# Neighbourhood attention in pairs of heads, with products between its turns

## The chip, the cores and the metric

One core of a Trainium2 chip runs the kernel. The metric is the device time of one execution in microseconds. The kernel before took 3163.59 us (median of three runs, 3157.02 to 3165.70).

## The reference, cut to what matters

The program runs two blocks over 256 latent tokens `x` and 256 context tokens, with 1024 features, everything in fp32. The first block has two layers of SwiGLU feed-forward, a mixer, and feed-forward again. The second block has two layers: latent attention (8 heads) with an MLP, and neighbourhood attention (16 heads of 64) with an MLP. The change touches the two attentions, and the order of the feed-forward tiles. Neighbourhood attention is:

```python
s_lat = jnp.einsum('bqhd,bkhd->bhqk', q_row, k_strip).astype(jnp.float32) * scale + bias
s_lat = jnp.where(mask, s_lat, -jnp.inf)
s_ctx = jnp.einsum('bqhd,bkhd->bhqk', q_row, kc).astype(jnp.float32) * scale
p = jax.nn.softmax(jnp.concatenate([s_ctx, s_lat], -1), axis=-1).astype(v.dtype)
return jnp.einsum('bhqk,bkhd->bqhd', p, jnp.concatenate([vc, v_strip], 1))
```

The grid has 4 rows of 64 columns, so the strip is the whole latent sequence; the bias comes from a table of relative positions per head. The output of all heads goes through `w_o`. Latent attention is a softmax attention over context and latent keys, with query, key and value made from low-rank vectors (`uq`, `uk`, and `mla_v`) and a rotary part.

## The kernel before, in words

All activations lie feature-major: 8 tiles of 128 features by 512 tokens, context first. A weight is read as a slab of 128 x 1024 (SP's queue, seven slots), and split in two fp32r parts: high by ScalarE (L1300), low by VectorE (L1706). An activation has a high and a low part as well, and a product is three matmuls (L2192, L2193, L2194). A slab feeds 24 of them. `schedule` (L860) walks one hand-written order of steps, `order` (L736), and every engine's program takes its own steps out of it; so each engine works in that order, and waits by semaphores. When a slab is used up ("done"), the slab seven further is fetched and the slab five further is split.

In the feed-forward stages `ffn_pieces` (L464) makes the hidden tiles of a chunk (the sizes are in `SIZES`, L166), then the eight down products of that chunk, then the next chunk. The dot products of the modulation (two VectorE operations of 1024 elements each) are put between.

`beside` (L564) lays pieces of products between the turns of an attention: the turn's steps, then the copies of the piece before ("late"), then the products of one piece, then the next unit's scores. `pair_turns` (L680) gives turns of a pair of heads: turn i normalises unit i-1, transposes unit i-2, and weighs the values when a pair's last unit is through. For latent attention (`mla_steps`, L697) a unit is a pair of heads and one tile of 128 queries: scores of both heads in two of three banks (L2542, and the rotary part with the rows 0 to 63 and 64 to 127 of the array, L2545), max by VectorE (L2104), exponential by ScalarE (L1606), reciprocal and scaling by VectorE (L2110, L2114), transposes by TensorE (L2367), copy by ScalarE (L1626), weighing (L2394). Its pieces have the banks 4 and 5: `both` (L693) joins two products into one piece, and the list is

```python
pieces = [both(*q1), both(uk[0], uk[1]), both(uk[2], uk[3]), both(*q2), both(*q3), v[0], v[1], None, None, None, None, *outs]
```

with 19 turns for 19 entries; `outs` is the half of the output product over the first four feature tiles.

For neighbourhood attention, the keys (`na_k`), queries (`na_q`) and all values (`na_tm`, copied with their bias by VectorE at L1861) are made first. `na_steps` (L729) then runs 32 units, one head and 128 queries each, with `skewed`:

```python
yield from skewed(32, ("na_scores", "na_normalise", None, None, "na_turn"), more)
```

A unit: scores of one head in 64 rows of the array (L2555); ScalarE copies the context half with the scale (L1634); VectorE scales the latent half and adds the bias into SBUF (L2126), and takes the max (L2119); ScalarE's exponential (L1613); reciprocal by VectorE (L2134); scaling by POOL (L1232); four transposes (L2348) and a copy (L1462). Each second unit weighs the head's values (L2384, one bank per parity), ScalarE copies the result (L1479), and for each second head its high and low parts are made (L1359, L1784). The bias of a head is loaded by two DMAs of SP (L1116), reversed by a POOL copy (L1244) and masked by a second POOL operation (L1246), one head ahead of its use. The output product (`na_out`, 8 slabs) follows behind the last head, with the residual added by VectorE (L1833).

## Time and profile before

| | |
|---|---|
| median of three runs | 3163.59 us |
| profiled execution | 3168.26 us |
| its span | 3166.5 us |
| TensorE matmul busy | 2887.7 us (91%) |
| TensorE weight load busy | 2367.5 us (75%) |
| VectorE busy | 1975.9 us (62%) |
| ScalarE busy | 1174.8 us (37%) |
| POOL busy | 417.7 us (13%) |
| mean granted TensorE clock | 0.946 |

Busy times overlap, and a matmul's end is modelled, so the busy share of TensorE says only whether it had work. The stretches in the section with the rows are cut by hand from the start of a stage's first matmul to the start of what follows its last. PEclk is the clock that TensorE was granted, as a share of 2.4 GHz.

### The profile page before, as it was taken

What the parts mean: (1) busy time and instruction counts of PE and PEld (TensorE: products, weight loads), DVE (VectorE), ACT (ScalarE), POOL (GpSimd) and SP (SyncE); (2) the same over time, 40 slices, a digit from 0 to 9 for tenths busy, and PEclk for the clock granted to TensorE, in tenths of its full rate; (3) what the DMA queues carried; (4) which work ended last, traced back from release to release, by engine and by line L of the source; (5) the groups of instructions that cost most, each with busy time, mean ns of one, the idle gap of its engine ahead of it and who ended that gap; (6) DMA issues with size and microseconds to landing.
All of it is one profiled execution on the core that took longest, in us unless ns stands there. A gap on an engine that the chain in (4) does not pass through costs nothing.

```text
span 3166.5 us, 38256 instructions
## 1 busy us (share of the span) xinstructions
PE 2887.7 (91%) x15166; PEld 2367.5 (75%) x15166; DVE 1975.9 (62%) x3242; ACT 1174.8 (37%) x1953; POOL 417.7 (13%) x460
## 2 busy tenths in 40 slices
PE   3899999988899998999998799988899998988797
PEld 2788887545788887888887699855678887845797
DVE  7888855645678857878555765533566764433554
ACT  3222234443422234232355554423442223335552
POOL 0000010322100010000101110100310003035201
PEclk7999999978999999999999899988999999989898
DMA  6555522101355634555332255310144432332353
GB/s 245 193 193 206 180 85 87 54 27 40 137 196 194 213 110 163 199 199 200 107 105 67 67 187 187 114 53 20 60 140 160 162 138 73 107 76 41 130 187 107
DMA packets 125281, 412.13 MB, mean 130 GB/s; under 512 B 25088, under 2 KB 27136, under 8 KB 124464
## 3 DMA queue, kind: packets, MB, share of 16 engines
q1 hardware_dynamic: 109552, 353.07, 33.0%
q0 software_dynamic: 15552, 56.63, 5.1%
q8 instruction: 120, 1.97, 0.2%
q14 instruction: 57, 0.47, 0.0%
HBM read 408.60 MB, written 1.05 MB: 129 GB/s over the span
## 4 chain that ended last, share of the span: by engine, by line
PE 80%; DVE 8%; ACT 7%; issue 2%; POOL 2%; DMA 1%; POOLq 0%; SPq 0%; ACTq 0%; DVEq 0%
PE bank L2192 25%; PE bank L2193 24%; PE bank L2194 24%; PE bank L2394 2%; POOL sb_temp L1168 1%; DVE sb_split_low L1706 1%; ACT sb_split_high L1300 1%; DVE sb_temp L1770 1%; DVE sb_temp L1720 1%; DVE sb_h_low L1776 1%; DVE sb_rstd L1762 1%; PE bank L2384 1%; ACT sb_temp L1613 1%; PE bank L2542 1%; ACT sb_x_res L1370 1%
## 5 line engine op out<-in xcount | busy, mean ns | idle before, releaser
L2192 PE MATMUL bank<-sb_h_high,sb_split_high 128*128 128x256 f32 (+1 forms) x3040 | 1066.6, 351 | 119.6 <-DVE sb_h_low L1776 47.9
L2193 PE MATMUL bank<-sb_h_low,sb_split_high 128*128 128x256 f32 (+1 forms) x3040 | 1042.8, 343 | 0.0
L2194 PE MATMUL bank<-sb_h_high,sb_split_low 128*128 128x256 f32 (+1 forms) x3040 | 1041.7, 343 | 0.0
L1706 DVE TENSOR_TENSOR sb_split_low<-sb_raw,sb_split_high 128x1024 fp32r<-128x1024 f32 x515 | 636.1, 1241 | 231.9 <-ACT sb_split_high L1300 228.3
L2192 PEld LDWEIGHTS bank<-sb_h_high,sb_split_high 128*128 128x128 f32 x3040 | 592.1, 195 | 213.4 <-issue 69.8
L1300 ACT ACTIVATE sb_split_high<-sb_raw 128x1024 fp32r<-128x1024 f32 x515 | 536.6, 1051 | 344.9 <-DMA sb_raw<-weights 344.8
L2193 PEld LDWEIGHTS bank<-sb_h_low,sb_split_high 128*128 128x128 f32 x3040 | 594.0, 195 | 67.2 <-issue 0.5
L2194 PEld LDWEIGHTS bank<-sb_h_high,sb_split_low 128*128 128x128 f32 x3040 | 593.0, 195 | 68.1
L1720 DVE CUSTOM_DVE_ANT_0 sb_temp<-sb_ada_ffn,sb_cond_ffn 128x1024 bf16<-128x1024 f32 x408 | 479.2, 1218 | 12.0 <-ACT sb_cond_ffn L1304 7.9
L1833 DVE SCALAR_TENSOR_TENSOR sb_x_res<-bank,sb_gates,sb_x_res 128x256 f32<-128x256 f32 x312 | 140.1, 477 | 265.5 <-PE bank L2194 265.2
L2192 PE MATMUL bank<-sb_hidden_high_ffn,sb_split_high 128*128 128x512 f32 (+1 forms) x788 | 272.7, 346 | 0.0
L2193 PE MATMUL bank<-sb_hidden_low_ffn,sb_split_high 128*128 128x512 f32 (+1 forms) x788 | 272.1, 345 | 0.0
L2194 PE MATMUL bank<-sb_hidden_high_ffn,sb_split_low 128*128 128x512 f32 (+1 forms) x788 | 272.0, 345 | 0.0
L1378 ACT ACTIVATE sb_temp<-bank 128x256 f32<-128x256 f32 (+1 forms) x163 | 80.3, 493 | 362.0 <-PE bank L2194 361.9
L1391 ACT ACTIVATE sb_hidden_high_ffn<-sb_temp 128x512 fp32r<-128x512 f32 (+1 forms) x94 | 52.1, 555 | 356.2 <-DVE sb_temp L1811 356.2
L2192 PE MATMUL bank<-sb_hidden_high_mlp,sb_split_high 128*128 128x256 f32 (+1 forms) x552 | 180.9, 328 | 0.0
L2193 PE MATMUL bank<-sb_hidden_low_mlp,sb_split_high 128*128 128x256 f32 (+1 forms) x552 | 180.5, 327 | 0.0
L2194 PE MATMUL bank<-sb_hidden_high_mlp,sb_split_low 128*128 128x256 f32 (+1 forms) x552 | 180.4, 327 | 0.0
L1148 POOL DMA_DIRECT2D sb_ada_ffn<-ada x90 | 47.8, 532 | 897.1 <-DVE sb_ada_col L1720 897.1
L2193 PEld LDWEIGHTS bank<-sb_hidden_low_ffn,sb_split_high 128*128 128x128 f32 x788 | 148.3, 188 | 19.9
L2192 PEld LDWEIGHTS bank<-sb_hidden_high_ffn,sb_split_high 128*128 128x128 f32 x788 | 148.3, 188 | 19.9
L2194 PEld LDWEIGHTS bank<-sb_hidden_high_ffn,sb_split_low 128*128 128x128 f32 x788 | 148.3, 188 | 19.8
(265 smaller groups left out, 3088.9 us busy)
## 6 DMA issues: line engine op xcount, KB each, us to landing
sb_raw<-weights SPq DMA_DIRECT2D x515, 512.0 KB, 3.3
sb_ada_ffn<-ada SPq DMA_DIRECT2D x114, 512.0 KB, 4.3
sb_ada_ffn<-ada POOLq DMA_DIRECT2D x90, 512.0 KB, 3.5
sb_ada_mlp<-ada POOLq DMA_DIRECT2D x18, 512.0 KB, 3.4
sb_ada_mlp<-ada SPq DMA_DIRECT2D x18, 512.0 KB, 4.2
sb_cond_ffn<-cond SPq DMA_DIRECT2D x3, 1024.0 KB, 5.1
sb_na_raw<-na_rpb SPq DMA_DIRECT2D x32, 96.0 KB, 5.8
sb_x_res<-tokens SPq DMA_DIRECT2D x1, 2048.0 KB, 15.2
```

The source lines that it names most:

```text
L1148: lane.do.dma_start(m.ada[f][i][:, :], m.w["ada"][n, :, :]).then_inc(*lane.mark(ada_signal(n), n, step=16))
L1168: do.tensor_tensor(acc, other if k == 1 else acc, new, ALU.add).then_inc(*pool.mark("added", (kind, tag, k, p)))
L1300: do.activation(m.high[s % SLOTS][:, :], m.raw[s % SLOTS][:, :], identity).then_inc(*act.mark("split_high", s))
L1378: do.activation(m.temp[h % 2][:, COLS[p]], src, func).then_inc(*act.mark(name, (f, h, p)))
L1391: do.activation(m.hidden[f][i][:, m.hidden_cols(f, p)], m.temp[h % 2][:, COLS[p]], identity).then_inc(*act.mark("hidden_high", (f, h, p)))
L1706: do.tensor_tensor(m.low[i][:, :], m.raw[i][:, :], m.high[i][:, :].bitcast(F32), ALU.subtract).then_inc(*dve.mark("split_low", s))
L1720: do.tensor_tensor_reduce(out=m.junk(s), in0=m.ada[f][i][:, :], in1=m.cond[f][:, s, :], scale=1.0, scalar=0.0, op0=ALU.mult, op1=ALU.add, ...
L1833: do.scalar_tensor_tensor(x, m.bank[bank][:, bank_cols(p, s)], m.gates[:, k, s:s + 1], x, ALU.mult, ALU.add).then_inc(*dve.mark("x_new", ( ...
L2192: do.matmul(out, ah, bh, start=start and j == 0, stop=False)
L2193: do.matmul(out, ah, bl, start=False, stop=False)
L2194: last = do.matmul(out, al, bh, start=False, stop=stop and j == len(terms) - 1)
L2394: last = do.matmul(m.bank[bank][:, c], vals[:, kt, col + hd * P:col + (hd + 1) * P], m.big[stage][:, at + kt, c], start=kt == 0, stop=kt = ...
```

## The change

- Neighbourhood attention runs in `pair_turns` as latent attention does: 16 units of two heads and 128 queries in 19 turns. The scores of both heads are in different rows of the array and in two of three banks; the query's scale is applied where the query is copied (all by VectorE). VectorE adds the bias in place in PSUM, takes the max from PSUM, and scales by the reciprocal; POOL has no part in it any more. The two heads of a pair are weighed in one bank, in alternating matmuls on different output columns, with one copy of 128 partitions.
- The bias of a pair is loaded (four DMAs) one turn ahead of the turn that makes it, which VectorE does with one operation for each head, reversed and masked at once.
- Before the turns: five query slabs and half the values (`na_v0`). Between the turns: three query slabs, the other values (`na_v1`, eight pieces of two slabs and one token tile), an empty entry, and the output product over the first four feature tiles. Behind: its second half. The first four tiles of the attention's result are put as high and low parts in turn 11.
- Latent attention: `uq` 1 goes ahead of the turns, each piece has one bank, the value pieces take one token tile; the slabs' order follows, and four tiles of the result may be put earlier (`H_LAST_FIRST`).
- Feed-forward in chunks: the first hidden tile of the next chunk is made before the down products (`AHEAD`), with one more buffer for a hidden tile.

```diff
-          ("mla_uk1", 1), ("mla_uq2", 2), ("mla_v1", 1), ("mla_out", 8), ("mlp0", 64),
-          ("na_fm", 16), ("na_tm", 8), ("na_out", 8), ("mlp1", 64)]
+          ("mla_uq2", 2), ("mla_uk1", 1), ("mla_v1", 1), ("mla_out", 8), ("mlp0", 64),
+          ("na_k", 8), ("na_q", 5), ("na_v0", 4), ("na_q5", 3), ("na_v1", 4), ("na_out", 8), ("mlp1", 64)]
 N_SLABS = sum(n for _, n in STREAM)
+AHEAD = 1
...
-      "na_tm": (NA_V, 0, 4, (0, 1))}
-OUT_HALVES = {"even_out": (4, 0), "odd_out": (0, 4), "mla_out": (0, 4)}
+      "na_v0": (NA_V, 0, 4, (0,)), "na_v1": (NA_V, 0, 4, (1,))}
+OUT_HALVES = {"even_out": (4, 0), "odd_out": (0, 4), "mla_out": (0, 4), "na_out": (0, 4)}
...
+def ups_at(f, c):
+    return min(chunk_at(f, c) + AHEAD, sum(SIZES[f])) if c else 0
 def down_slab(f, c, block):
-    return SLAB0[f] + chunk_at(f, c + 1) * n_up(f) + chunk_at(f, c) + block // 8
+    return SLAB0[f] + ups_at(f, c + 1) * n_up(f) + chunk_at(f, c) + block // 8
+def n_hidden(f):
+    return max(SIZES[f]) + (AHEAD if len(SIZES[f]) > 1 else 0)
...
+H_LAST_FIRST = {"mla_y": (4, SLAB0["mla_uq2"] + 1)}
...
-        for h in range(chunk_at(f, c), chunk_at(f, c + 1)):
+        for h in range(ups_at(f, c), ups_at(f, c + 1)):
...
+def fm_signal(name, j):
+    return "fm_dve" if j % 2 or name == "na_q" else "fm_act"
...
+def tm_tile_pieces(name, g, n, ring):
+    k_slabs = TM[name][2]
+    first = SLAB0[name] + TM[name][3].index(g) * k_slabs
+    for tt in range(TT):
+        half, t = divmod(tt, 2)
+        bank = ring.next()
+        banks = (None, bank) if t else (bank, None)
+        for at in range(0, k_slabs, n):
+            yield [(kind, name, g, half, i, first + i, banks) for kind in ("tm", "tm_copy") for i in range(at, at + n)] + [
+                ("done", first + i) for i in range(at, at + n) if tt == TT - 1]
...
-    q0 = list(uq_pieces(0, ring))
+    q0, q1 = list(uq_pieces(0, ring)), list(uq_pieces(1, ring))
     yield from flat(pe)
     yield "rope", "mla_q", 0, 6
     yield "rope", "mla_q", 1, 7
     yield from q0[0]
     yield "rope", "mla_q", 2, 6
     yield "rope", "mla_q", 3, 7
-    yield from q0[1]
+    yield from flat([q0[1], *q1])
     ring = Ring(4, 2)
-    q1, uk, q2, q3 = list(uq_pieces(1, ring)), list(uk_pieces(1, ring)), list(uq_pieces(2, ring)), list(uq_pieces(3, ring))
-    v = list(tm_pieces("mla_v1", ring))
-    outs = [out_piece("mla_out", k, 0, BOTH, ring) for k in range(DT)]
-    pieces = [both(*q1), both(uk[0], uk[1]), both(uk[2], uk[3]), both(*q2), both(*q3), v[0], v[1], None, None, None, None, *outs]
+    q2, q3, uk = uq_pieces(2, ring), uq_pieces(3, ring), uk_pieces(1, ring)
+    pieces = [next(which) for which in (q2, uk, q2, uk, q3, q3, uk, uk)] + list(tm_tile_pieces("mla_v1", 1, 1, ring))
+    pieces += [out_piece("mla_out", k, 0, BOTH, ring) for k in range(DT)]
     yield from beside(list(pair_turns("mla", 4 * TT, TT)), pieces)
     yield from flat(pieces)
...
 def na_steps(ring):
-    yield from flat(tm_pieces("na_tm", ring))
-    yield "na_bias", 0
-    more = lambda u: ((("weigh", "na", u // 2),) if u % 2 else ())
-    yield from skewed(32, ("na_scores", "na_normalise", None, None, "na_turn"), more)
+    yield from flat(tm_pieces("na_v0", ring))
+    ring = Ring(4, 2)
+    pieces = [*(fm_piece("na_q", j, LAT_PART, ring) for j in range(5, 8)), *tm_tile_pieces("na_v1", 1, 2, ring), None]
+    pieces += [out_piece("na_out", k, 0, LAT_PART, ring) for k in range(DT)]
+    units = list(pair_turns("na", 16, 2))
+    for t in range(1, 8):
+        units[2 * t - 2][0].append(("na_rpb", t))
+        units[2 * t - 1][0].append(("na_bias", t))
+    units[11][0].extend(("na_put", k) for k in range(4))
+    yield from beside(units, pieces)
+    yield from flat(pieces)
...
+    yield "na_rpb", 0
...
     yield from flat(head[1])
     yield from flat(body)
-    yield from flat(fm_pieces("na_q", ring, 0)[1])
+    yield "na_bias", 0
+    yield from flat(fm_pieces("na_q", ring)[1][:5])
     yield from na_steps(ring)
-    body, _ = out_pieces("na_out", ring, 0)
+    ring = Ring(0, 6)
     yield "scales", "p11"
-    yield from flat(body)
+    yield from flat([out_piece("na_out", k, 1, LAT_PART, ring) for k in range(DT)])
...
+    def na_rpb(pair):
+        rpb, n_r, n_c = w["na_rpb"], 15, 31
         sp.wait_ge(*REGION["na"])
-        if hd >= 2:
-            sp.wait_ge("bias_flip", hd - 2)
-        for r2 in range(2):
-            at = bass.AP(rpb.tensor, hd * n_r * n_c + (4 + r2) * n_c + 15 - (GRID_W - 1), [[1, GRID_W], [n_c, NA_REL], [1, GRID_W]])
-            do.dma_start(raw[r2 * GRID_W:(r2 + 1) * GRID_W, :].rearrange("p (m n) -> p m n", n=GRID_W), at).then_inc(
-                *sp.mark(f"rpb{hd % 2}", (hd, r2), step=16))
-    def na_scores(u):
-        if u % 2 == 0 and u // 2 + 1 < 16:
-            na_bias(u // 2 + 1)
+        for c in range(2):
+            hd, raw = 2 * pair + c, m.na_raw[c]
+            if pair:
+                sp.wait_ge("na_bias", hd - 2)
+            for r2 in range(2):
+                at = bass.AP(rpb.tensor, hd * n_r * n_c + (4 + r2) * n_c + 15 - (GRID_W - 1), [[1, GRID_W], [n_c, NA_REL], [1, GRID_W]])
+                do.dma_start(raw[r2 * GRID_W:(r2 + 1) * GRID_W, :].rearrange("p (m n) -> p m n", n=GRID_W), at).then_inc(
+                    *sp.mark(f"rpb{c}", (hd, r2), step=16))
...
-    def normalise(kind, u, n):
-        temp, col = m.temp[u % 6], m.cols[u % 6]
-        pool.wait_ge("recip", (kind, u))
-        do.tensor_scalar(temp[:, 0:n], temp[:, 0:n], col[:, 2:3], None, ALU.mult).then_inc(*pool.mark("normalised", (kind, u)))
-    def na_normalise(u):
-        normalise("na", u, T)
-    def na_bias(hd):
-        raw, bias, n_b = m.na_raw[hd % 2], m.na_bias[hd % 2], NA_REL * GRID_W
-        mask = m.C("na_mask").rearrange("p (o n) -> p o n", o=1).broadcast_to([P, NA_REL, GRID_W])
-        by_row = bias[:, :].rearrange("p (m n) -> p m n", n=GRID_W)
-        pool.wait_ge(f"rpb{hd % 2}", (hd, 1))
-        if hd >= 2:
-            pool.wait_ge("na_lat", 2 * hd - 3)
-        do.tensor_copy(bias[:, :], raw[:, n_b - 1::-1]).then_inc(*pool.mark("bias_flip", hd))
-        pool.wait_ge("bias_flip", hd)
-        do.tensor_tensor(by_row, by_row, mask, ALU.add).then_inc(*pool.mark("bias_mask", hd))
-    def na_scores(u):
-        if u % 2 == 0 and u // 2 + 1 < 16:
-            na_bias(u // 2 + 1)
...
+    def na_put(tile):
+        act.wait_ge("weigh_copy", ("na", 2 * tile + 1))
+        put_high("na_y", tile, LAT_PART, m.na_q[:, tile, :])
     def weigh(kind, hd):
         act.wait_ge("weighed", (kind, hd))
         if kind == "na":
-            base, tile = HD * (hd % 2), hd // 2
-            do.activation(m.na_q[base:base + HD, tile, :], m.bank[5 + hd % 2][base:base + HD, 0:NX_TOK], identity).then_inc(
-                *act.mark("weigh_copy", (kind, hd)))
-            if base:
-                act.wait_ge("weigh_copy", (kind, hd))
-                put_high("na_y", tile, LAT_PART, m.na_q[:, tile, :])
+            if hd % 2:
+                do.activation(m.na_q[:, hd // 2, :], m.bank[6][:, 0:NX_TOK], identity).then_inc(*act.mark("weigh_copy", (kind, hd)))
+                if hd >= 8:
+                    na_put(hd // 2)
...
+    def pair_scores(kind, u, n):
+        col = m.cols[u % 6]
+        for c in range(2):
+            act.wait_ge("maxed", (kind, u, c))
+            if u >= 3:
+                act.wait_ge("turned", (kind, u - 3, c))
+            do.activation(m.temp[2 * (u % 3) + c][:, 0:n], m.bank[(2 * u + c) % 3][:, 0:n], ACT.Exp, bias=col[:, c:c + 1],
+                          accum_out=col[:, 2 + c:3 + c]).then_inc(*act.mark("exped", (kind, u, c)))
...
-        do.activation(temp[:, CTX], m.bank[u % 3][:, CTX], identity, scale=HD ** -0.5).then_inc(*act.mark("na_ctx", u))
-        softmax("na", u, T)
...
+    def pair_max(kind, u, n):
+        col = m.cols[u % 6]
+        for c in range(2):
+            dve.wait_ge("na_biased" if kind == "na" else "scored", (kind, u, c))
+            do.tensor_reduce(col[:, c:c + 1], m.bank[(2 * u + c) % 3][:, 0:n], AX.X, ALU.max, negate=True).then_inc(
+                *dve.mark("maxed", (kind, u, c)))
     def mla_scores(u):
-        n, col = n_keys(u % TT), m.cols[u % 6]
+        pair_max("mla", u, n_keys(u % TT))
+    def na_bias(pair):
+        mask = m.C("na_mask").rearrange("p (o n) -> p o n", o=1).broadcast_to([P, NA_REL, GRID_W])
         for c in range(2):
-            dve.wait_ge("scored", ("mla", u, c))
-            do.tensor_reduce(col[:, c:c + 1], m.bank[(2 * u + c) % 3][:, 0:n], AX.X, ALU.max, negate=True).then_inc(
-                *dve.mark("maxed", ("mla", u, c)))
-    def mla_normalise(u):
-        n, col = n_keys(u % TT), m.cols[u % 6]
-        dve.wait_ge("exped", ("mla", u, 1))
-        do.reciprocal(col[:, 4:6], col[:, 2:4]).then_inc(*dve.mark("recip", ("mla", u)))
-        dve.wait_ge("recip", ("mla", u))
+            hd = 2 * pair + c
+            raw, bias = [t[:, :].rearrange("p (m n) -> p m n", n=GRID_W) for t in (m.na_raw[c], m.na_bias[hd % 4])]
+            dve.wait_ge(f"rpb{c}", (hd, 1))
+            if pair >= 2:
+                dve.wait_ge("na_biased", ("na", 2 * pair - 3, c))
+            do.tensor_tensor(bias, raw[:, ::-1, ::-1], mask, ALU.add).then_inc(*dve.mark("na_bias", hd))
+    def na_scores(u):
+        at = (2 - 2 * (u % 2)) * GRID_W
+        for c in range(2):
+            hd, bank = 2 * (u // 2) + c, m.bank[(2 * u + c) % 3]
+            dve.wait_ge("na_bias", hd)
+            dve.wait_ge("scored", ("na", u, c))
+            do.tensor_tensor(bank[:, LAT], bank[:, LAT], m.na_bias[hd % 4][:, at:at + NX_TOK], ALU.add).then_inc(
+                *dve.mark("na_biased", ("na", u, c)))
+        pair_max("na", u, T)
+    def pair_normalise(kind, u, n):
+        col = m.cols[u % 6]
+        dve.wait_ge("exped", (kind, u, 1))
+        do.reciprocal(col[:, 4:6], col[:, 2:4]).then_inc(*dve.mark("recip", (kind, u)))
+        dve.wait_ge("recip", (kind, u))
         for c in range(2):
             temp = m.temp[2 * (u % 3) + c][:, 0:n]
-            do.tensor_scalar(temp, temp, col[:, 4 + c:5 + c], None, ALU.mult).then_inc(*dve.mark("weights", ("mla", u, c)))
-    def maxed(kind, u, src, n):
-        if u >= 6:
-            dve.wait_ge("normalised", (kind, u - 6))
-        do.tensor_reduce(m.cols[u % 6][:, 0:1], src[:, 0:n], AX.X, ALU.max, negate=True).then_inc(*dve.mark("maxed", (kind, u)))
-    def na_scores(u):
-        hd, at = u // 2, (2 - 2 * (u % 2)) * GRID_W
-        temp = m.temp[u % 6]
-        dve.wait_ge("na_ctx", u)
-        dve.wait_ge("bias_mask", hd)
-        do.scalar_tensor_tensor(temp[:, LAT], m.bank[u % 3][:, LAT], HD ** -0.5, m.na_bias[hd % 2][:, at:at + NX_TOK],
-                                ALU.mult, ALU.add).then_inc(*dve.mark("na_lat", u))
-        dve.wait_ge("na_lat", u)
-        maxed("na", u, temp, T)
-    def normalise(kind, u):
-        col = m.cols[u % 6]
-        dve.wait_ge("exped", (kind, u))
-        do.reciprocal(col[:, 2:3], col[:, 1:2]).then_inc(*dve.mark("recip", (kind, u)))
+            do.tensor_scalar(temp, temp, col[:, 4 + c:5 + c], None, ALU.mult).then_inc(*dve.mark("weights", (kind, u, c)))
...
+    def na_weigh(pair):
+        vals = m.vals("na", NA_V)
+        wait_for_tm(f"na_v{pair // 4}")
+        free(6)
+        for c in range(2):
+            pe.wait_ge("turn_copy", ("na", 2 * pair + 1, c))
+        for kt in range(TT):
+            for c in range(2):
+                hd = 2 * pair + c
+                last = do.matmul(m.bank[6][HD * c:HD * c + HD, 0:NX_TOK], vals[:, kt, hd * HD:(hd + 1) * HD],
+                                 m.big["na"][:, NA_WT[c] + kt, LAT], start=kt == 0, stop=kt == TT - 1)
+        last.then_inc(*pe.mark("weighed", ("na", 2 * pair), ("na", 2 * pair + 1)))
+        read[6] = "weigh_copy", ("na", 2 * pair + 1)
...
     def na_scores(u):
-        hd, qt = u // 2, 2 + u % 2
-        base, tile = HD * (hd % 2), hd // 2
-        wait_for_fm(pe, "na_q")
+        tile, qt = divmod(u, 2)
+        wait_for_tile(pe, "na_q", tile)
         wait_for_fm(pe, "na_k")
-        free(u % 3)
-        do.matmul(m.bank[u % 3][:, :], m.na_q[base:base + HD, tile, (qt - 2) * P:(qt - 1) * P],
-                  m.big["na"][base:base + HD, NA_K + tile, :], start=True, stop=True).then_inc(*pe.mark("scored", ("na", u)))
-        read[u % 3] = "na_lat", u
+        for c in range(2):
+            free((2 * u + c) % 3)
+        for c in range(2):
+            bank, rows = (2 * u + c) % 3, slice(HD * c, HD * c + HD)
+            do.matmul(m.bank[bank][:, :], m.na_q[rows, tile, qt * P:(qt + 1) * P], m.big["na"][rows, NA_K + tile, :],
+                      start=True, stop=True).then_inc(*pe.mark("scored", ("na", u, c)))
+            read[bank] = "exped", ("na", u, c)
```

## Rows read from the trace of the kernel before

**Rows 1.** Windows: start:end, length, busy (x instructions) per engine, PEclk, DMA share, GB/s

```profile
2100.60:2249.00 148.40, 127.59 (x481) 81.99 (x480) 54.66 (x116) 54.30 (x129) 0.00 (x0) 0.91 0.09 29
2732.80:2755.40 22.60, 22.60 (x192) 22.55 (x191) 11.27 (x12) 9.42 (x12) 0.00 (x0) 1.00 0.53 179
2755.40:2800.60 45.20, 45.20 (x197) 36.19 (x195) 14.93 (x17) 8.54 (x9) 0.00 (x0) 1.00 0.29 97
2800.60:2915.40 114.80, 89.70 (x321) 41.68 (x320) 44.38 (x105) 61.29 (x151) 70.89 (x64) 0.90 0.27 33
2915.40:2938.00 22.60, 22.60 (x193) 22.58 (x192) 11.82 (x16) 9.07 (x10) 9.80 (x6) 1.00 0.48 163
```

**Rows 2.** Waits of 2800 to 2917 us: engine, line, releaser, total us, times, longest

```profile
ACT sb_temp L1613 <- DVE sb_cols L2119: 45.0, 32, 7.5
POOL sb_temp L1232 <- DVE sb_cols L2134: 31.3, 23, 2.9
...
PE bank L2555 <- DVE sb_temp L2126: 7.7, 1, 7.7
```

**Rows 3.** Waits of PE, 2096 to 2262 us

```profile
PE bank L2192 <- ACT sb_mla_big L1597: 7.0, 3, 2.8
PE bank L2192 <- DVE sb_mla_big L2098: 5.9, 2, 3.5
...
PE bank L2192 <- DVE sb_mla_big L1864: 3.0, 1, 3.0
```

**Rows 4.** Windows of two of the four feed-forward stages that run in chunks

```profile
832.00:1191.00 359.00, 358.79 (x1655) 294.35 (x1655) 265.69 (x409) 98.91 (x128) 26.32 (x39) 1.00 0.51 179
...
2316.00:2656.00 340.00, 340.00 (x1596) 281.43 (x1597) 224.51 (x346) 102.75 (x137) 23.66 (x34) 0.99 0.44 150
```

**Rows 5.** Timeline of PE, latent attention: start, us, engine, line, operation, count

```profile
2200.55 1.88 PE L2542 MATMUL bank<-sb_mla_big 128*128 128x512 f32 x4
2202.36 1.13 PE L2545 MATMUL bank<-sb_mla_big 64*128 64x512 f32 x4
2203.42 1.09 PE L2367 MATMUL bank<-sb_const,sb_temp 128*128 128x128 f32 x8
2204.27 0.48 PE L2192 MATMUL bank<-sb_h_high,sb_split_high 128*128 128x512 f32 x1
...
2207.15 1.02 PE L2542 MATMUL bank<-sb_mla_big 128*128 128x256 f32 x4
...
2214.06 2.85 PE L2394 MATMUL bank<-sb_mla_big 128*128 128x512 f32 x8
...
2220.34 0.60 PE L2367 MATMUL bank<-sb_const,sb_temp 128*128 128x128 f32 x4
```

**Rows 6.** Timeline of PE, neighbourhood attention

```profile
2856.00 1.94 PE L2384 MATMUL bank<-sb_na_big 128*64 128x256 f32 x8 [0.75 <-ACT sb_na_big L1462]
2857.87 1.12 PE L2555 MATMUL bank<-sb_na_big,sb_na_q 64*128 64x512 f32 x2
```

**Rows 7.** Timeline of DVE and ACT, one full turn of latent attention

```profile
2203.52 1.29 DVE L2104 TENSOR_REDUCE sb_cols<-bank 128x1 f32<-128x512 f32 x2 [2.87 <-PE bank L2545]
...
2205.59 1.08 ACT L1626 ACTIVATE sb_mla_big<-bank 128x512 f32<-128x512 f32 x2
...
2205.93 0.89 DVE L2114 TENSOR_SCALAR sb_temp<-sb_temp,sb_cols 128x512 f32<-128x512 f32 x2
```

**Rows 8.** Groups of DVE by line and shape

```profile
L1706 DVE TENSOR_TENSOR sb_split_low<-sb_raw,sb_split_high 128x1024 fp32r<-128x1024 f32 x515 | 636.1, 1241 | 231.9 <-ACT sb_split_high L1300 228.3
...
L2126 DVE SCALAR_TENSOR_TENSOR sb_temp<-bank,sb_na_bias 128x256 f32<-128x256 f32 x32 | 13.5, 422 | 26.4 <-ACT sb_temp L1634 18.9 <-POOL sb_na_bias L1246 7.2
...
L1861 DVE TENSOR_TENSOR sb_na_big<-bank,sb_na_bv 128x512 f32<-128x512 f32 x8 | 5.5, 690 | 21.9 <-PE bank L2194 21.9
```

**Rows 9.** Tile na_raw: issues on SP and landing

```profile
L1116 SPq DMA_DIRECT2D sb_na_raw<-na_rpb x32: 595/626/660, 2801.1 to 2887.9; - x32
...
DMA to landing us min/median/max: 4.9/5.8/6.5
```

194 lines of the change are left out of this document (94 added, 100 removed).

## The prediction

> **What bounds the kernel now.** I read the windows first, to find the two stages that the change rebuilds, then the waits inside each, then the timelines of single turns. Latent attention's turns run from 2100.6 to 2249.0 us, 148.4 us [rows 1]. The neighbourhood mixer takes 22.6 us for queries, 45.2 for values, 114.8 for attention and 22.6 for its output [rows 1], 205.2 in all. In the last two projections and the values TensorE is busy all the time at full clock; in the two attention windows its mean clock is 0.91 and 0.90, and it is idle for 20.8 and 25.1 us. So these windows hold waiting, and half-clock stretches that the waiting leaves behind.
>
> In neighbourhood attention one (head, 128 queries) unit goes round scores, part copy, bias, max, exponential, POOL normalise, transposes, copy; the waits are spread over this ring: 45.0 us of ScalarE for the max, 31.3 of POOL for the reciprocal [rows 2]. At its start TensorE stands 7.7 us for the first bias [rows 2], whose loads are issued only when the values are done. Nothing else is there for TensorE to do. In latent attention the pieces between turns do the filling, but TensorE waits 7.0 + 5.9 + 3.0 = 15.9 us, in six waits, for the copy that empties a piece's bank [rows 3]: `both` puts two pieces into one turn, the ring has two banks, and the copies come a turn later.
>
> **Latent attention: -24 us.** No work is removed; pieces of `uq` 1 go ahead of the turns, every turn gets a piece of one bank, and the last output piece follows behind. I add up the same work at full clock without bank waits [rows 5]. A piece of 12 matmuls of 512 columns takes 2207.15 - 2204.27 = 2.88 us; there are 14 (six `uq`, eight outputs), and eight of half that size (keys, values): 51.8. A unit with 512 keys: scores 2203.42 - 2200.55 = 2.87 and transposes 0.85, times 8 = 29.8; a unit with 256 keys is taken as half, 14.9. A pair's weighing, 2220.34 - 2214.06 = 6.28 with its short wait for the shared bank, times 4 = 25.1. Sum 121.6 against 148.4: 26.8, of which 15.9 are the waits and the rest the clock. Bounds: 15.9 if the clock stays as it is, 26.8 if all comes back; nothing is added, so I see no loss unless the waits return. A vector-engine turn, from the first max to the last normalise, is 2206.82 - 2203.52 = 3.3 us [rows 7], under TensorE's shortest full turn with a piece, 2.87 + 0.85 + 1.44 = 5.2. Other waits will be met now and then; I take 24.
>
> **Neighbourhood attention: -48 us.** The new work, step by step.
> Queries 0 to 4 at 22.6 / 8 = 2.82 us a slab: 14.1. Half the values, 22.6. The first bias is loaded one stage earlier and made under the key and query products, so the 7.7 us go.
> Then 19 turns of a pair of heads. TensorE's terms: scores of both heads 1.06, because the rows 0 to 63 and 64 to 127 of the array already work side by side in latent attention: four 64-row instructions take 2203.42 - 2202.36 = 1.06 us [rows 5], as long as one head's two take here, 1.12 [rows 6]. Transposes 0.85 [rows 5]. Weighing: one head's eight instructions take 2857.87 - 2856.00 = 1.87 us [rows 6]. The new loop alternates the two heads on different output columns of the array; no row shows that. It costs 1.87 if they run side by side, 3.74 if not; I take 1.87, as the nearest row, the two row halves, does overlap. Piece: 2.82 for a query or a value piece, 1.41 for an output piece. The value pieces hold four slabs until their last token tile.
> VectorE's terms for a turn: two bias adds in PSUM, 0.42 each as the add that it does now [rows 8], and the 3.3 of rows 7: 4.14. In odd turns to 13 the next pair's bias: 2 x 384 elements in one operation with mask and reversed order, between 0.42 (256) and 0.69 (512) [rows 8], so 1.1 together. Late steps: a split 1.24, a value copy 0.69 [rows 8], a low part 0.42 like the other operations of 256 elements, a query copy or residual add 0.45 (an estimate just above it).
> The larger of the two sets a turn, since the banks and temporaries let one run ahead of the other by about a turn:
> turn 0: 2.82 + 1.06 = 3.9 (TensorE).
> Turns 1 to 3: VectorE, 3 x 4.14 + 2 x 1.1 + 3 x (0.45 + 1.24) = 19.7; TensorE would need 14.
> Turns 4 to 9: TensorE, 6.60 with weighing and 4.73 without, three times: 34.0; VectorE needs some 30.
> Turn 10: 6.6 for either. Turn 11: VectorE 10.1, with bias, four low parts, a copy and two splits at once, and TensorE has no piece.
> Turns 12 to 15: VectorE, 4 x 4.14 + 1.1 + 2 x 0.42 + 3 x 0.45 + 1.24 = 21.1.
> End: last unit's softmax 4.14, transposes 0.85, the two copies 1.08 [rows 7], weighing 1.87, two output pieces 2.82: 10.8.
> Together 106.2 us. The other output half, 8 x 1.41 = 11.3; the last tiles are ready behind the two pieces. 14.1 + 22.6 + 106.2 + 11.3 = 154.2 against 205.2: 51 us less. In the VectorE-bound turns TensorE pauses a few us each and half-clock stretches will return; the unit's loop then has a doubled score time inside. I put 3 us on that and take 48.
> The POOL work (70.9 us in this window [rows 1]) leaves the ring; it was partly its price. ScalarE has two exponentials, two copies and at most one split a turn, under 5 us. SP: a pair's four loads, 0.63 us of issue each and 5.8 to landing [rows 9], 8.3 us plus the bias itself, about 9.4 for a pair, against pair turns of 11.3: hidden, with 2 us to spare. The residual adds come twice for each tile, 8 x 0.45 more on VectorE, counted above. In the final half POOL's row sums have 1.41 us a tile in place of 2.82; one output slab's split and the adds fit, so nothing is charged.
>
> **Feed-forward chunks: 0.** One hidden tile of the next chunk is made before the down products at nine chunk boundaries. Nothing waits there: TensorE is busy 358.8 of 359 and 340.0 of 340 us [rows 4]. What covers a hidden tile's chain now is the other tiles of its chunk, and the change lengthens that. Without cover, each boundary would pay about one chain of 2 to 3 us. The slab order changes with the work order, so the splits keep their distance. Bounds: 0 gain, 9 us loss.
>
> **Sum.** 24 + 48 = 72 us. The profiled execution took 3168.3 us (span 3166.5); minus 72 is 3096. It lies 4.7 above the median of the three runs, 3163.6, from which the same sum gives 3092. I say 3094.
>
> **Rivals.**
> (a) The weighing of two heads is not side by side. Then the four TensorE-bound turns with weighing and the end pay 1.87 each: +9, 3103. The one form of this kernel with 64 output columns [rows 6] shows one head at a time, so the rows leave it open. The Trainium skill (TensorEngine Tiling (Array Packing), Key Properties) says that tiles operate independently, loads and matmuls in parallel; by it the weighing costs 1.87. The same page (Restrictions and Gotchas) says that column tiling excludes fast weight load, and a load-bound pair would cost more than 1.87, towards (a).
> (b) VectorE's turn is longer than I add up, through the add in place in PSUM or the reversed bias: at 0.69 an add and double the bias, 1.6 us on the turns that VectorE sets and half on the others, about +13: 3107. For it: every turn passes four PSUM operations through VectorE. Against: the present add reads PSUM at 0.42.
> (c) The one-bank pieces don't do what they say: the copy still comes too late and latent attention keeps its 148.4 us: 3118. Against: a bank is used again two turns later, the copy comes one turn later.
> (d) Slower: the bias loads. They sit on SP's queue, may start only when VectorE has flipped the previous pair, and VectorE then waits for them ahead of the scores of its turn. If a pair's four land one after another, 4 x 5.8 + 0.6 + 1.1 = 24.9 us a pair, 174 for seven pairs in place of the 84 us of turns 0 to 13: 3184. It eats the whole gain from about 22 us a pair on. Against: now 32 loads land within some 90 us, which needs at least two in flight.
>
> **Chances.** Forecast 0.55, (a) 0.20, (b) 0.13, (c) 0.06, (d) 0.03, and 0.03 for a feed-forward loss or something else that leaves little. The range goes from 3082 (all of the clock back, 6 us below for the spread of runs) to 3120, which holds (a), (b), their sum and (c). A difference of 0.3% (9.5 us) is about what a measurement can tell. Faster 0.94, same 0.03, slower 0.03.
>
> **What would show it.** Latent attention's turns in about 124 us with no PE wait released by L1597, L2098 or L1864 and a clock near 1.0. The stretch from the first query product to the last output product in 154 to 158. The weighing of a pair x16 in 1.9 us, or 3.7. VectorE with little idle in turns 1 to 3 and 11 to 15 and a long turn 11. Bias operations that never wait for a load. Wrong, if a DMA releases VectorE, if PE's waits sit on the transposes in every turn, or if the feed-forward windows are longer than before.

## The result, and the profile after

The changed kernel took **3086.3 us** (median of four runs, 3085.0 to 3088.1), the kernel before 3161.6 beside it: ratio 0.976, 95% interval 0.975 to 0.978. The forecast was 3094, the range 3082 to 3120. The profiled executions are 3168.26 and 3085.08 us (spans 3166.5 and 3083.3), 83.2 apart where the medians are 75.3 apart; the stages below account for the former. The clock over the span is 0.952 for 0.946, TensorE 2834.8 us busy for 2887.7, POOL 344.1 for 417.7.

The windows of the changed kernel, cut at the same products as [rows 1, 4]: latent attention, five query slabs, half the values, the turns, the second half of the output; then the turns in three parts, and one of the two feed-forward stages (columns as in [rows 1]).

```profile
2101.20:2215.50 114.30, 111.13 (x469) 71.00 (x468) 53.57 (x116) 52.59 (x127) 0.00 (x0) 1.00 0.10 33
2697.90:2712.00 14.10, 14.10 (x121) 14.05 (x120) 9.28 (x12) 4.16 (x4) 0.00 (x0) 1.00 0.56 180
2712.00:2734.70 22.70, 22.70 (x101) 18.32 (x101) 7.18 (x8) 5.47 (x6) 0.00 (x0) 1.00 0.28 98
2734.70:2844.70 110.00, 95.70 (x588) 67.86 (x587) 76.66 (x161) 55.54 (x125) 0.00 (x0) 0.95 0.36 78
2844.70:2855.80 11.10, 11.08 (x95) 10.88 (x93) 7.97 (x13) 3.27 (x4) 6.79 (x6) 1.00 0.56 189
...
2734.70:2757.00 22.30, 18.43 (x113) 14.72 (x111) 13.77 (x26) 6.98 (x16) 0.00 (x0) 0.92 0.59 128
2757.00:2803.00 46.00, 43.95 (x245) 28.72 (x244) 32.59 (x71) 22.40 (x54) 0.00 (x0) 1.00 0.31 46
2803.00:2844.00 41.00, 32.63 (x225) 23.72 (x226) 29.62 (x63) 25.47 (x57) 0.00 (x0) 0.92 0.29 89
...
832.00:1191.00 359.00, 357.78 (x1648) 292.99 (x1646) 265.79 (x407) 98.43 (x129) 26.34 (x39) 1.00 0.52 180
```

Latent attention takes 114.3 us for 148.4 (-34.1), the neighbourhood mixer 157.9 for 205.2 (2697.9 to 2855.8, -47.3). The feed-forward windows hold as much TensorE work as before, within about 1 us (358.8 and 340.0 us busy before, 357.8 and 340.0 now). 34.1 + 47.3 = 81.4 of the 83.2; of the other stretches, that ahead of latent attention is 0.6 longer, that between the two attentions 1.4 shorter and that behind 1.0 shorter. POOL is empty in both attentions.

What TensorE waits for in the latent window (first line) and in 2695 to 2850 us; engine, line, releaser, total us, times, longest:

```profile
PE bank L2444 <- ACT sb_mla_big L1511: 3.1, 4, 0.8
...
PE bank L2608 <- ACT sb_temp L1631: 4.2, 2, 2.5
PE bank L2227 <- DVE sb_na_q L1863: 3.9, 1, 3.9
PE bank L2425 <- DVE sb_na_big L1883: 3.7, 1, 3.7
```

The six waits of [rows 3] are gone, 15.9 us; what is left is 0.8 for each pair's shared bank, as before. In the turns two single waits stand out, 3.9 us for a query copy and 3.7 for a copy of values. VectorE's timeline of turn 11 shows where the second comes from:

```profile
2801.43 0.76 DVE L2149 TENSOR_TENSOR bank<-bank,sb_na_bias 128x256 f32<-128x256 f32 x2
...
2805.29 1.19 DVE L2141 TENSOR_TENSOR sb_na_bias<-sb_na_raw,sb_const 128x384 f32<-128x384 f32 x2
2806.39 1.42 DVE L1802 TENSOR_TENSOR sb_h_low<-sb_na_q,sb_h_high 128x256 fp32r<-128x256 f32 x4
2807.74 0.68 DVE L1883 TENSOR_TENSOR sb_na_big<-bank,sb_na_bv 128x512 f32<-128x512 f32 x1
2808.34 2.43 DVE L1724 TENSOR_TENSOR sb_split_low<-sb_raw,sb_split_high 128x1024 fp32r<-128x1024 f32 x2
2810.69 0.76 DVE L2149 TENSOR_TENSOR bank<-bank,sb_na_bias 128x256 f32<-128x256 f32 x2
```

From one pair of bias adds (2801.43) to the next (2810.69) are 9.3 us. The last value copy stands in that queue behind the low parts of four tiles, and the weighing of the fifth pair, the first that needs it, behind the copy. TensorE's timeline at two weighings:

```profile
2770.13 1.95 PE L2425 MATMUL bank<-sb_na_big 128*64 128x256 f32 x16
2772.00 1.09 PE L2405 MATMUL bank<-sb_const,sb_temp 128*128 128x128 f32 x8
...
2808.52 3.68 PE L2425 MATMUL bank<-sb_na_big 128*64 128x256 f32 x16 [3.66 <-DVE sb_na_big L1883]
```

A pair is weighed in 1.87 us, start to start, as long as one head took before [rows 6]. The same x16 behind the wait takes 3.61 us, nearly twice that: from 2808.5 to 2812.1 us the granted clock is 0.50, the lower of its two levels, 1.2 GHz.

VectorE's waits from 2735 to 2850 us:

```profile
...
DVE sb_na_bias L2141 <- DMA sb_na_raw<-na_rpb: 3.4, 1, 3.4
```

And its groups there (line, operation, shapes, count; busy us, mean ns; idle before):

```profile
L2149 DVE TENSOR_TENSOR bank<-bank,sb_na_bias 128x256 f32<-128x256 f32 x32 | 12.1, 424 | 7.6 <-PE bank L2608 7.6
L2141 DVE TENSOR_TENSOR sb_na_bias<-sb_na_raw,sb_const 128x384 f32<-128x384 f32 x14 | 7.3, 552 | 3.5 <-DMA sb_na_raw<-na_rpb 3.4
```

One bias operation, that of turn 1, waited 3.4 us for its load; twelve later ones did not. This row was named ahead as one that would speak against the forecast's step on the loads. The four loads that it waited for, and the times from their issue to their landing:

```profile
L1166 SPq DMA_DIRECT2D sb_na_raw<-na_rpb x4: 617/625/626, 2735.1 to 2737.1; - x4
DMA to landing us min/median/max: 5.4/7.1/9.4
```

Before, such a load took 5.8 us in the median and 6.5 at most [rows 9]. Here a slab fetch was issued right behind the four, at 2737.8, and landed 10.0 us later, where a slab takes 3.3 us as a rule.

### The profile page after: what moved, and what is told of

It is laid out like the page before. It is cut to its first block, busy times and chain, and to the rows that moved or that the text cites. A ratio compares the mean times of both kernels' runs of the same rounds, so it can differ in the third digit from the quotient of the medians.

```text
span 3083.3 us, 38159 instructions
## 1 busy us (share of the span) xinstructions
PE 2834.8 (92%) x15166; PEld 2343.9 (76%) x15166; DVE 1995.1 (65%) x3286; ACT 1156.8 (38%) x1909; POOL 344.1 (11%) x396
## 4 chain that ended last, share of the span: by engine, by line
PE 81%; DVE 8%; ACT 6%; issue 2%; POOL 2%; DMA 1%; SPq 0%; POOLq 0%; ACTq 0%; DVEq 0%
PE bank L2227 25%; PE bank L2228 24%; PE bank L2229 24%; PE bank L2444 2%; POOL sb_temp L1214 1%; DVE sb_split_low L1724 1%; ACT sb_split_high L1322 1%; DVE sb_temp L1788 1%; DVE sb_temp L1738 1%; DVE sb_h_low L1794 1%; DVE sb_rstd L1780 1%; PE bank L2592 1%; DMA sb_na_raw<-na_rpb 1%; PE bank L2405 1%; ACT sb_x_res L1392 1%
## 5 line engine op out<-in xcount | busy, mean ns | idle before, releaser
L1738 DVE CUSTOM_DVE_ANT_0 sb_temp<-sb_ada_ffn,sb_cond_ffn 128x1024 bf16<-128x1024 f32 x408 | 479.2, 1218 | 12.7 <-ACT sb_cond_ffn L1326 8.1
L1829 DVE TENSOR_TENSOR sb_temp<-sb_temp,bank 128x512 f32<-128x512 f32 (+1 forms) x94 | 55.5, 590 | 152.0 <-PE bank L2229 152.0
```

The lines of the kernel that those rows point to most:

```text
L1738: do.tensor_tensor_reduce(out=m.junk(s), in0=m.ada[f][i][:, :], in1=m.cond[f][:, s, :], scale=1.0, scalar=0.0, op0=ALU.mult, op1=ALU.add, ...
L1829: do.tensor_tensor(temp, temp, src, ALU.mult).then_inc(*dve.mark("hidden_raw", (f, h, p)))
```

## The experiments

Twelve kernels ran, in three groups of four, each group on one chip and beside the kernel before. Experiments 1 to 4 were one group and are set against the first result, 3086.3. In the other two groups (experiments 5, 6 and 9; 7, 8 and 10) the changed kernel ran unaltered as well, 3089.9 and 3089.3, and the three others of the group are set against that. Line numbers shift by one or two between kernels. The time of "the turns" is from the start of the first scores to the start of the last weighing matmul.

**1. Feed-forward without the tile ahead**

```diff
-AHEAD = 1
+AHEAD = 0
```

> The changed kernel with the feed-forward order of before (no hidden tile ahead of the down products). My theory: nothing waited at a chunk boundary, so this part is worth nothing; time within 3 us of the changed kernel's 3086, the first feed-forward body as long as with it (345 us). Rival (the extra tile gave cover at nine boundaries, 1 to 3 us each): 3095 to 3113, with TensorE waits on the hidden tiles.

3090.9 us (3085.1 to 3092.8), ratio 0.977 [0.976, 0.979]; the profile has the same span as the change's, 3083.3. The median is 4.7 us over the first result, more than the 3 us expected, but 1.0 and 1.6 over the two later medians of the same changed kernel (3089.9 and 3089.3). So the reordering of hidden tiles is worth nothing that can be measured, in either direction.

**2. The changed kernel with latent attention as before**

```diff
-    pieces = [next(which) for which in (q2, uk, q2, uk, q3, q3, uk, uk)] + list(tm_tile_pieces("mla_v1", 1, 1, ring))
-    pieces += [out_piece("mla_out", k, 0, BOTH, ring) for k in range(DT)]
+    pieces = [both(*q1), both(uk[0], uk[1]), both(uk[2], uk[3]), both(*q2), both(*q3), v[0], v[1], None, None, None, None, *outs]
```

(with `uq` 1, the slabs' order and `H_LAST_FIRST` as before)

> The changed kernel with latent attention's pieces, slab order and turns as before. Theory: the 34.1 us between the two traces in this window are this part's alone; 3120, with six TensorE waits of 15.9 us together and a clock near 0.91 in the window. Rival (my predicted size of 24 us was right and the rest came from elsewhere, as the one output piece moved behind the turns): 3110.

3114.4 us (3111.5 to 3117.0), ratio 0.985 [0.984, 0.987]: 28 us more than the changed kernel (24.5 more than its runs in the second group), between the 3120 of the theory and the 3110 of its rival. The waits come back to a tenth of a us, as in [rows 3]:

```profile
PE bank L2228 <- ACT sb_mla_big L1622: 7.0, 3, 2.8
PE bank L2228 <- DVE sb_mla_big L2121: 5.9, 2, 3.5
...
PE bank L2228 <- DVE sb_mla_big L1887: 3.0, 1, 3.0
```

But the window is 140.5 us (2098.9 to 2239.4), not 148.4, and its mean clock 0.96, not 0.91. The difference is the clock. Windows of 20 us, first of the kernel before, then of this one, whose later windows all have 1.00:

```profile
2100.00:2120.00 20.00, 15.43 (x54) 10.36 (x54) 5.49 (x13) 4.50 (x13) 0.00 (x0) 0.83 0.13 41
2120.00:2140.00 20.00, 13.74 (x51) 8.87 (x50) 7.00 (x13) 7.06 (x16) 0.00 (x0) 0.88 0.10 39
2140.00:2160.00 20.00, 17.64 (x67) 12.35 (x65) 4.74 (x9) 5.38 (x15) 0.00 (x0) 0.86 0.08 27
2160.00:2180.00 20.00, 16.39 (x53) 9.30 (x53) 6.03 (x13) 6.68 (x15) 0.00 (x0) 0.83 0.08 27
2180.00:2200.00 20.00, 17.55 (x68) 10.45 (x67) 9.10 (x22) 10.40 (x28) 0.00 (x0) 0.91 0.00 0
```

```profile
2100.00:2120.00 20.00, 12.12 (x52) 7.47 (x52) 8.41 (x20) 7.45 (x20) 0.00 (x0) 0.97 0.16 52
2120.00:2140.00 20.00, 17.05 (x55) 12.14 (x56) 5.31 (x9) 4.34 (x9) 0.00 (x0) 0.78 0.08 27
```

A mean of 0.83 over 20 us is 20 x 2 x 0.17 = 6.8 us at 1.2 GHz. By that sum the kernel before spent some 28 us of its window at the lower level and this one 10, with the same six waits. Half of such time is lost: 14 us and 5, a difference of 9 for the 7.9 between the windows. The profile of the kernel before is also of an unlucky execution: its 3168.26 us lie above every other execution of that kernel beside these runs (3157.0 to 3166.4).

**3. The kernel before with the latent part alone.** The edit is the reverse of experiment 2, made on the kernel before.

> The kernel before with the latent attention of the changed kernel and nothing else. Theory: the two attention parts add up; 34 us less than before, 3127, window of 114 us. Rival (the parts share something, as the place of a slab or a throttled stretch): the gain differs from that of undoing it in the changed kernel by over 5 us.

3135.0 us (3134.0 to 3136.7), ratio 0.992 [0.990, 0.993], 26.7 us less than the kernel before beside it. From the first scores to the last weighing 108.2 us, to a tenth those of the changed kernel (2101.2 to 2209.4), against 145.4 before (5.8 us of that are a `uq` and an output piece that the 108.2 do not hold). The 3135.0 is 8 us over the 3127 expected, because that figure took the 34 us from the two profiles. The two parts of the change add up: 26.7 here, and 3161.8 - 3114.4 = 47 for all that is not latent attention, 74 together, for the 75 measured.

**4. A pair weighed one head after the other**

```diff
-        for kt in range(TT):
-            for c in range(2):
+        for c in range(2):
+            for kt in range(TT):
```

> The changed kernel with the eight weighing matmuls of a pair issued head by head and not alternating; nothing else differs. Theory: alternation lets the two column halves work side by side; without it a weighing takes 3.7 us and not 1.87, and the TensorE-bound turns with weighing (4, 6, 8, 10) and the end pay it: 7 to 9 us more, 3094. Rival (the halves overlap in either order, as the array's queue looks past one instruction): 3086 and 1.9 us.

3096.3 us (3095.1 to 3099.3), 10.0 over the changed kernel, 6.4 over its runs in the second group. The row of one pair, and what follows it:

```profile
2776.22 2.86 PE L2425 MATMUL bank<-sb_na_big 128*64 128x256 f32 x16
2779.02 1.09 PE L2405 MATMUL bank<-sb_const,sb_temp 128*128 128x128 f32 x8
```

2.80 us a pair, start to start, for 1.87 with alternated heads. So alternating does make the column halves run side by side. In turn they don't cost the full double, 3.74 (an estimate, 2 x 1.87): half of the second head's time is still saved. The turns take 108.6 us, where the unaltered kernel's three profiles have 103.2, 104.0 and 104.8: 3.8 to 5.4 more, as five of the eight weighings, those of turns 4, 6, 8 and 10 and the last, would give, 5 x 0.93 = 4.7. The rest of the 10.0 isn't the weighing's: in this profile the first scores start 5.6 us later than in the changed kernel's (2743.1 and 2737.5), and up to there the two programs are the same. Rival (a) is out for the order that the change has.

**5. Pairs without pieces between the turns.** Query slabs 5 to 7 and the second half of the values ahead of the turns, the first output half behind them.

```diff
-    pieces = [*(fm_piece("na_q", j, LAT_PART, ring) for j in range(5, 8)), *tm_tile_pieces("na_v1", 1, 2, ring), None]
-    pieces += [out_piece("na_out", k, 0, LAT_PART, ring) for k in range(DT)]
+    yield from flat([fm_piece("na_q", j, LAT_PART, ring) for j in range(5, 8)])
+    yield from flat(tm_pieces("na_v1", ring))
+    pieces = []
```

> The changed kernel, but all query, value and output products of neighbourhood attention stand ahead of or behind the 19 turns, with nothing between turns. It divides the gain in the pairs' own and the overlap's. Theory: the bare turns are set by VectorE, 4.14 us a turn and 5.1 with a bias, about 16 x 4.6 + 9 = 83 us in place of 114.8, and the 42 us of products come on top: 42 + 83 = 125 against 106 in the changed kernel; 3105. Rival (the pairs alone gain little, overlap is all): 115 us of turns, 3137.

3103.8 us (3100.8 to 3105.6), 13.9 over the unaltered kernel. The turns take 82.3 us from first to last matmul, where the 32 units took 114.5: 32 us of the gain come without any piece between the turns, 14 from the work laid there, out of 42 us of pieces. The 32 are two heads a turn, no POOL, no copy of the context half, and the first bias, which is now made before the turns: for it alone TensorE had stood 7.7 us [rows 2], inside the 114.5.

**6. Bias a turn earlier, its load right behind the first bias** 

```diff
-        units[2 * t - 2][0].append(("na_rpb", t))
-        units[2 * t - 1][0].append(("na_bias", t))
+        if t > 1:
+            units[2 * t - 3][0].append(("na_rpb", t))
+        units[2 * t - 2][0].append(("na_bias", t))
...
     yield "na_bias", 0
+    yield "na_rpb", 1
```

> The changed kernel with each pair's bias loaded and made one turn earlier (in the turns with weighing, where TensorE is the longer), the second pair's loads right behind the first bias. Theory: the 3.4 us wait for the load in turn 1 and one bias of 1.0 us in a VectorE-bound turn go: 3 to 5 us less than the unaltered kernel of this call. Rival (turns 10 and 12 now pay what turns 11 and 13 save, and something else ends turn 1): no difference.

3090.8 us (3089.0 to 3092.9), no different from the unaltered 3089.9, where 3 to 5 us less were expected. The turns do get shorter, 99.2 us for 103.2 to 104.0, but the stages ahead get longer. In turn, the window of the queries and values, the wait of ScalarE and that of TensorE in it:

```profile
2700.00:2748.00 48.00, 44.11 (x246) 38.25 (x245) 18.43 (x23) 10.81 (x10) 0.00 (x0) 0.93 0.39 113
```

```profile
ACT sb_split_high L1324 <- DMA sb_raw<-weights: 35.6, 9, 15.5
...
PE bank L2229 <- DVE sb_na_q L1865: 3.9, 1, 3.9
```

These stages ran with TensorE busy all the time before [rows 1] and in the change, and ScalarE waited 28.3 us for weights there in the unaltered kernel beside it. Here TensorE stands for 3.9 us and falls to the lower clock, because a split, and behind it on VectorE the query copy, waits for a slab (ScalarE stood 12.4 us for it). SP holds its issues in order: the load for the second pair waits for the first bias add on VectorE, and the weight fetches stand behind it. That alone puts them off by some 2 us (the fetches around the loads are 5.0 us apart, for 2.8 in the unaltered kernel). More comes behind the issue. The next two slab fetches:

```profile
L1131 SPq DMA_DIRECT2D sb_raw<-weights x2: 903/1408/1912, 2707.5 to 2708.4; - x2
...
DMA to landing us min/median/max: 11.7/11.8/12.0
```

In the unaltered kernel the slabs of this stage land 3.2 to 3.4 us after their issue. The four loads are of 96 KB each and go in small packets: from 2700 to 2722 us, 1685 packets of under 512 B for 96 without them. Loads and fetches share one DMA queue; why the one holds up the other there isn't shown.

**7. The same, with that load issued later**, at the start of the values:

```diff
 def na_steps(ring):
+    yield "na_rpb", 1
```

> As e7_bias_early (the bias tiles of each pair of heads a turn earlier), but the loads for the second pair are issued at the start of the stage of values, not right behind the first pair's bias add, so that SyncE's queue of weight loads isn't held back. Theory (the 3.45 us that VectorE waited for na_raw in turn 1 lie on the path, and e7's loss came from the weights behind a wait on SyncE): the turns take 99 to 101 us as in e7, the stage ahead of them stays as in the unaltered kernel, and the time is 3 to 5 us under the yardstick. Rival (TensorE's work sets the end of the turns and the wait is made up later, or the weights are late for another reason): within 2 us of the yardstick.

The loads are now issued from 2716.3 to 2718.6 us, behind a slab fetch with none to follow for 11 us, and land in 5.4 to 6.5 us.

3083.3 us (3081.1 to 3084.3) against 3089.3 (3085.4 to 3091.9): 6.0 us less, and less than any run of the unaltered kernel. The turns take 98.7 us for 104.8 beside it. Waits of TensorE and VectorE, as above:

```profile
PE bank L2427 <- DVE sb_na_big L1885: 2.1, 1, 2.1
PE bank L2229 <- DVE sb_na_q L1865: 1.9, 1, 1.9
...
DVE sb_na_bias L2143 <- DMA sb_na_raw<-na_rpb: 1.4, 2, 1.1
```

Beside it, the unaltered kernel waits 4.7 us for loads, 3.8 for the query copy behind them and 4.9 for the value copy (whose turn has no bias in it any more here). So the turns held 6 us that the bias's place gives back, and experiment 6 had lost in SP's queue and behind it what it won in the turns. How much of the 6 us is the load's wait isn't divided.

**8. The bias made by GpSimd**

```diff
-            do.tensor_tensor(bias, raw[:, ::-1, ::-1], mask, ALU.add).then_inc(*dve.mark("na_bias", hd))
+            do.tensor_tensor(bias, raw[:, ::-1, ::-1], mask, ALU.add).then_inc(*pool.mark("na_bias", hd))
```

(in GpSimd's program, with the same waits)

> The add that makes the bias tile (128x384, 16 of them at 0.5 us on VectorE) is made by GpSimd, with the same waits; GpSimd has nothing else to do there. Theory (VectorE is the bound of turns 1 to 3 and 11 to 15, the load's 3.45 us block its queue, and an add on GpSimd beside it costs VectorE little): the 3.45 us and the four to eight adds in turns of VectorE go, 4 to 7 us under the yardstick, and the turns take 97 to 100 us for 103. Rival (GpSimd's add with its reversed rows is slower, by more than a turn, or slows VectorE's own operations where the two run at once): the same time within 2 us, or a few us slower, with VectorE waiting for GpSimd.

3083.5 us (3078.9 to 3086.6), 5.8 less; the turns take 97.9 us. Two of its groups:

```profile
L1284 POOL TENSOR_TENSOR sb_na_bias<-sb_na_raw,sb_const 128x384 f32<-128x384 f32 x14 | 13.1, 940 | 124.0 <-DMA sb_na_raw<-na_rpb 94.1 <-DVE bank L2149 29.8
...
L2160 DVE TENSOR_SCALAR sb_temp<-sb_temp,sb_cols 128x512 f32<-128x512 f32 x32 | 15.1, 513 | 0.6
```

An operation costs GpSimd 0.94 us in the mean, and 0.86 where nothing holds it, for VectorE's 0.55, but now it is GpSimd that waits for the loads. VectorE's scaling goes from 484 to 513 ns in the mean, 1.0 us in all. The timelines of POOL and VectorE show two places where it was held, and a third where GpSimd was:

```profile
2742.76 0.87 POOL L1284 TENSOR_TENSOR sb_na_bias<-sb_na_raw,sb_const 128x384 f32<-128x384 f32 x1 [71.59 <-DMA sb_na_raw<-na_rpb]
2750.33 1.76 POOL L1284 TENSOR_TENSOR sb_na_bias<-sb_na_raw,sb_const 128x384 f32<-128x384 f32 x1 [2.43 <-DMA sb_na_raw<-na_rpb]
2764.89 0.87 POOL L1284 TENSOR_TENSOR sb_na_bias<-sb_na_raw,sb_const 128x384 f32<-128x384 f32 x1 [2.27 <-DMA sb_na_raw<-na_rpb]
```

```profile
2742.41 1.50 DVE L2160 TENSOR_SCALAR sb_temp<-sb_temp,sb_cols 128x512 f32<-128x512 f32 x2
2765.23 1.21 DVE L2160 TENSOR_SCALAR sb_temp<-sb_temp,sb_cols 128x512 f32<-128x512 f32 x2
2770.04 0.88 DVE L2160 TENSOR_SCALAR sb_temp<-sb_temp,sb_cols 128x512 f32<-128x512 f32 x2
```

The two pairs of operations that met GpSimd's add took 1.50 and 1.21 us, the next 0.88: 0.95 us more together, nearly all of the 1.0. The add at 2750.33 began while a split of VectorE ran (2750.14 to 2751.37) and took 1.76 us for 0.86. The Trainium skill (SBUF — State Buffer, "SBUF: two separate sides") says that GpSimd and VectorE share a pair of ports as an exclusive lock, when VectorE's operation is in a mode that takes two ports or, against a GpSimd operation that reads SBUF, has two SBUF inputs; the one that starts later then waits for the whole instruction of the other. The trace agrees in kind, in both directions: the waits are 0.3 to 0.9 us, no longer than what was left of the other's operation. Experiments 7 and 8 remove the same blocked queue by two ways; each was run alone, not both together.

**9. Each maximum of neighbourhood attention twice**

```diff
             if kind == "na":
+                do.tensor_reduce(col[:, 6 + c:7 + c], m.bank[(2 * u + c) % 3][:, 0:n], AX.X, ALU.max, negate=True)
```

> The changed kernel with each of the 32 max operations of neighbourhood attention done twice (the second result is not used), 0.6 us more on VectorE for each, 1.2 a turn. It shows which turns VectorE sets. Theory: turns 1 to 3 and 11 to 15 pay in full, turns 4 to 10 the part over VectorE's slack of some 1.7 us a pair: 11 to 13 us more. Rival (TensorE sets most turns): under 5. Rival (VectorE sets every turn): 19.

3101.8 us (3097.3 to 3105.6), 12.0 over the unaltered kernel. The turns grow from 104.0 us beside it to 114.7. The added operations are 21.8 us of VectorE; a bit over half of it reached the time. That is what a stage gives in which VectorE sets a part of the turns and TensorE the rest; had VectorE set none, or all, it would have been 0 or 22. The start of each turn's scores in the two profiles says where: counted from the first scores, those of turn 5 come 2.5 us later than without the added operations, those of turn 10 3.5, and the last weighing 10.7. So turns 6 to 10 took in all but 1.0 us of it, and from turn 11 on 7.2 were paid.

**10. Latent attention with only its keys in pieces of two banks**

```diff
-    pieces = [next(which) for which in (q2, uk, q2, uk, q3, q3, uk, uk)] + list(tm_tile_pieces("mla_v1", 1, 1, ring))
+    pieces = [q2[0], both(uk[0], uk[1]), q2[1], both(uk[2], uk[3]), q3[0], q3[1]] + list(tm_tile_pieces("mla_v1", 1, 1, ring))
```

> Only the pieces of keys between the turns of latent attention are of two banks again (two pieces of two banks for four of one; queries of one bank stay). Theory (each wait before a two-bank piece is for the copy of its second bank, which the turn that stands between can no longer hide): two waits of TensorE come back, of some 2.4 and 3.5 us, before scores, and the stretch from scores(0) to the end of the first half of the output grows from 114.3 us to 120 or 124, with up to 4 us more if the granted clock falls behind the waits; the time is 6 to 10 us over the yardstick. Rival (the waits hang on the order of queries and keys, not on the size of the piece): fewer than 2 us of waits, no difference of the time over 3 us.

3106.8 us (3102.6 to 3109.2), 17.5 over the unaltered kernel, where 6 to 10 were expected: the mechanism came as expected, at twice the price. The stretch from the first scores to the end of the first output half takes 130.0 us (2105.8 to 2235.8) for 114.3, 15.7 more. TensorE's waits in 2105 to 2240 us:

```profile
PE bank L2228 <- DVE sb_mla_big L2121: 6.0, 2, 3.0
PE bank L2228 <- ACT sb_mla_big L1622: 3.5, 2, 2.1
...
PE bank L2228 <- DVE sb_h_low L1803: 1.0, 1, 1.0
```

Four waits, not two: with a ring of two banks a piece that takes both makes its neighbour wait as well, the query piece behind it for the key copy, the key piece for the query copy. They come to 9.5 us. The granted clock is 0.89, 0.86 and 0.89 in 2105 to 2120, 2120 to 2140 and 2140 to 2160; by the sum of experiment 2 that is 13 us at the lower level, which cost half of it, 6.7. 9.5 + 6.7 = 16.2 for the 15.7 of the stretch, and 1.0 more for a low part just behind it: nearly the whole 17.5. One thing more differs than the pieces' size: the banks are dealt out list by list here and not in the order of the pieces, so that the first key product takes the very bank of the query piece before it. What a deal in order would save wasn't tried.

**The unaltered kernel again.** Once in each of the last two groups:

> The changed kernel once more, unaltered, on the chip and in the rounds of the three beside it: 3083 to 3091 us. Its distance to the others is what those are read from.

> The changed kernel, unaltered, as the yardstick of this call: between 3085 and 3091 us, as in the two runs of it so far (3086.3 and 3089.9).

3089.9 us (3087.6 to 3091.6) and 3089.3 (3085.4 to 3091.9). With the first result's 3086.3, the medians of one and the same kernel lie 3.6 us apart, so differences under about 4 us between groups say nothing here. Single profiles differ no less: in these three the first scores of latent attention start at 2101, 2103 and 2105 us.

## Why the prediction was right, step by step

**The sum.** 24 + 48 = 72 us was forecast, 75.3 measured between medians (83.2 between the two profiled executions; 26.7 for latent attention by experiment 3 and 47 for the rest by experiment 2). The two terms stand differently.

**Latent attention, -24: right in mechanism, mis-sized.** Forecast: the six waits go, and most of the half clock. In the traces it gave 34.1 us, in the medians 26.7 (experiment 3) and 24.5 to 28 (experiment 2). Two things failed in the term.
First, the sum of full-clock work, 121.6, counted six `uq` pieces. Between the first scores and the end of the first output half the kernel before makes four and the changed one three. The two of `uq` 1 stand ahead of the first scores in both: before, they were the first entry of the list, and an entry's products come before the scores of its turn. The changed kernel has the first piece of `uq` 2 there as well; the windows hold 481 and 469 matmuls [rows 1], and 12 are a piece. So the sum to set beside 148.4 was 121.6 - 2 x 2.88 = 115.8, and for the changed kernel it is 113.0, where 114.3 was measured. The gain that "all comes back" allowed was thus 148.4 - 115.8 = 32.6 and not 26.8, and one piece more only moved ahead of the window. The windows from the first rotary product to the first scores, before and after, show that move:

```profile
2047.50:2100.60 53.10, 43.91 (x160) 32.27 (x159) 25.38 (x31) 16.26 (x24) 7.67 (x10) 0.87 0.17 58
```

```profile
2045.10:2101.20 56.10, 47.60 (x171) 34.96 (x170) 26.40 (x32) 18.13 (x26) 7.65 (x10) 0.85 0.18 63
```

3.0 us longer, for 2.9 of work; experiment 2 has 53.0 there. So latent attention's own gain in the profiles is 34.1 - 3.0 = 31.1 us: the six waits 15.9, a wait of 1.7 for the exponential at 2182 us that is gone too, and half of the 27.6 at half clock, 13.8, make 31.4. "No work is removed" was right, but the forecast's sum was of work that the window didn't hold.
Second, the clock. The forecast took the profile before at its word. Experiment 2 shows that with the same waits the half-clock time can be 10 us or 28, which is 5 to 14 us of loss. So how much came back seems to hang on the execution that is looked at (two profiles, of two kernels with this stage in common, show it). The medians' 26.7 lies inside the stated bounds of 15.9 to 26.8, 2.7 above the 24, and there is luck in that: a sum too small by 5.8 stood against a profile that lost more to the clock than most executions.

**The one-bank ring** is why the waits went, and not the order of the pieces: experiment 10 keeps the order and brings back four waits with keys alone. Rival (c), the waits stay, is out.

**Neighbourhood attention, -48: right, 47.3 in the traces.** By its parts, forecast and then measured:

| | forecast | measured |
|---|---|---|
| queries 0 to 4 | 14.1 | 14.1 |
| half the values | 22.6 | 22.7 |
| turns and their end | 106.2 + 3 for the clock | 110.0 |
| second output half | 11.3 | 11.1 |

The turns, cut where VectorE starts the bias adds of units 0, 3, 10, 11 and 15 (2738.7, 2760.9, 2801.4, 2810.7 and 2832.0 us):

| | forecast | measured |
|---|---|---|
| turn 0 | 3.9 | 4.0 |
| turns 1 to 3 | 19.7 | 22.1 |
| turns 4 to 10 | 40.6 | 40.6 |
| turn 11 | 10.1 | 9.3 |
| turns 12 to 15 | 21.1 | 21.3 |
| end | 10.8 | 12.7 |

The TensorE-bound turns are the best: a turn with weighing was put at 6.60 and one without at 4.73, 11.3 for two, and from 2770.1 to 2781.8 such a pair took 11.6. VectorE's terms: two adds in PSUM 0.76 for 0.84, the two bias operations 1.0 to 1.2 for 1.1, the turn with four low parts 9.3 for 10.1 (copy and two splits in it, as told). Over the 106.2 came 3.8 us, about the 3 that were allowed for the clock, but elsewhere: 2.4 in turns 1 to 3, which hold the 3.4 us that VectorE stood for the load (the query copy that TensorE waited 3.9 for is next behind it in VectorE's queue), and 1.9 in the end. In turn 11 TensorE waited 3.66 us for the value copy and then worked at half clock, and turns 11 to 15 took no longer than forecast, since VectorE sets them. So the allowance was right in size by luck; the term that failed is the load's, which was put at nothing.

**VectorE as the bound of the outer turns.** Experiment 9's 12 us for 21.8 us of added work bears the split of the turns out: at 0.68 an added operation, two a turn, turns 1 to 3 and 11 to 15 alone would give 8 x 1.36 = 10.9, and the end 1.4 more. By turns the fit is rougher: from turn 11 on 7.2 us were paid, near the 8.2 of this sum, but 1.3 in turns 1 to 3 for 4.1 added, where the waits for loads shrank from 4.3 to 2.0 us and took in most of the difference. Rival (b) is out: an add in PSUM takes 424 ns [rows 8: 422 for the old form], and reversing costs nothing visible: 552 ns for 384 elements, between the 422 for 256 and the 690 for 512 of [rows 8].

**Rival (a), column halves in turn.** Experiment 4 decides it for alternated heads. The Trainium skill (TensorEngine Tiling (Array Packing), Key Properties) says that tiles operate independently; the alternated rows agree with 1.87 us, and the rows of one head after the other, 2.80, show that the order of issue decides how much of it one gets. The same page (Restrictions and Gotchas) says that column tiling excludes fast weight load. The prediction drew from it a pair dearer than 1.87; this trace shows no such cost, and one head alone, whose 1.87 the sum used, had 64 output columns too [rows 6].

**Rival (d), the loads.** It was given no more than 0.03, and loads one after another did not happen: 3.4 us once, not 12 a pair. But its mechanism was there in turn 1, where the second pair's loads are issued just one turn ahead. The step that failed is "hidden, with 2 us to spare", in two ways. It compared the load's 9.4 us with a pair of TensorE-bound turns, 11.3, and the first pair of turns is not one (turn 0 is 3.9). And it took 5.8 us to landing, where the last of these four took 9.4, with a slab fetch right behind it: issued at 2737.1, it would have landed at 2742.9 by the 5.8, just before VectorE came to it at 2743.2 (an estimate from [rows 9] and the timeline). Experiment 7 priced the bias's place at 6 us, together with the bias leaving the crowded turn 11; how the 6 splits between the two wasn't tried.

**Feed-forward: 0**, confirmed by experiment 1 and by the windows.

## What to carry to other kernels

Two-bank pieces in a two-bank ring make every piece wait a copy behind; one-bank pieces in every turn take the waits and the half clock after them away, and that half clock cost nearly as much as the waits in one profile here (13.8 and 15.9 us). When short turns go on several in-order queues, look at the queue's other customers: a load and a bias made one turn earlier paid 6 us where no slab fetch followed the load closely, and nothing where two did and landed 12 us after their issue. A load's time to landing is its time with the neighbours that it had where it was measured. When work is paired on halves of the array, alternate the halves instruction by instruction.

## What the runs showed of the hardware

- The same six waits of TensorE, equal to 0.1 us, were followed by some 28 us at 1.2 GHz in one profile and 10 in another (experiment 2, different kernels, same stage). So a cost of waiting worked out from one profile's clock may be off by 9 us here. What decides between the two stays open.
- Two heads' matmuls on different 64-column halves of the array: 1.87 us for a pair when alternated, 2.80 when issued one head after the other, 1.87 for a single head [rows 6].
- A slab of 512 KB lands 3.2 to 3.4 us after its issue in the query stage, and 11.7 to 12.0 us after it when four 96 KB loads in packets under 512 B stand right ahead of it on the same queue (experiment 6). The load with a slab fetch behind it took 9.4 us for a median of 5.8.
- GpSimd makes a 128x384 add with reversed rows in 0.86 us undisturbed for VectorE's 0.55. It held up VectorE's scaling by 1.0 us over 32 operations (0.88 to 1.50 and 1.21 for the two pairs shown), and was itself held by a split of VectorE, 1.76 us for 0.86.
